# Gated delta rule: the small triangular inverses of both directions in one block, with half as many products per level

## The reference

```python
def gated_delta_chunked(q, k, v, g, beta):
    ...
    G = jnp.cumsum(g, axis=-1)
    decay = jnp.where(incl, jnp.exp(diff), 0.0)
    kb = k * beta[..., None]
    a = jnp.where(strict, jnp.einsum('bhnid,bhnjd->bhnij', kb, k) * decay, 0.0)
    rhs = jnp.concatenate([v * beta[..., None], kb * jnp.exp(G)[..., None]], axis=-1)
    sol = lax.linalg.triangular_solve(a, rhs, left_side=True, lower=True, unit_diagonal=True)
    ...
    def step(state, inp):
        v_new = u_c - jnp.einsum('bhck,bhkv->bhcv', w_c, state)
        o_c = (jnp.einsum('bhck,bhkv->bhcv', qd_c, state)
               + jnp.einsum('bhij,bhjv->bhiv', intra_c, v_new))
        state = (state * jnp.exp(gl_c)[..., None, None]
                 + jnp.einsum('bhck,bhcv->bhkv', kd_c, v_new))
        return state, o_c
...
    o_fwd = gated_delta_chunked(qh, kh, vh, gh[0], bh[0])
    o_bwd = flip(gated_delta_chunked(flip(qh), flip(kh), flip(vh), flip(gh[1]), flip(bh[1])))
```

## Time and profile before

| what | us |
|---|---|
| median of 3 runs (lowest, highest) | 3313.6 (3311.71, 3314.68) |
| the profiled execution, its own time | 3314.71 |
| its span in the trace | 3312.9 |
| mean granted clock of PE, share of full speed | 0.964 |
| busy PE / PEld / DVE / ACT / POOL | 3097.8 / 2499.8 / 1645.6 / 1044.2 / 1142.9 |
| gdn_chunks, from its first instruction on POOL to the next stage | 225 to about 555 |

### The profile page before, as it was taken

The page is one execution under the profiler, slowest core; times in us unless marked ns, Lnnn a source line. Parts: engine busy times, 40 slices in busy tenths (PEclk is TensorE's granted clock), DMA queues, the critical chain, the costliest instruction groups (busy, mean ns, idle before and its releaser), DMA issues. The chain is left out here.

```text
span 3312.9 us, 55513 instructions
## 1 busy us (share of the span) xinstructions
PE 3097.8 (94%) x21758; PEld 2499.8 (75%) x21758; DVE 1645.6 (50%) x2424; ACT 1044.2 (32%) x1584; POOL 1142.9 (34%) x542
## 2 busy tenths in 40 slices
PE   8977887999999989999899899999999979999998
PEld 6845676788878767888578688888888544589987
DVE  7834443422131345421477657655555667367741
ACT  4322322312331443222331333222223434343332
POOL 4432211444444214444222022222232247534443
PEclk9988888999999989999899999999999989999999
DMA  4224334223223112232311111111111111122222
GB/s 146 94 96 169 125 112 167 88 95 96 100 89 115 51 34 94 90 100 96 105 46 56 56 52 63 63 63 63 64 63 58 49 42 44 43 82 89 95 89 82
DMA packets 80204, 275.49 MB, mean 83 GB/s; under 512 B 9500, under 2 KB 12380, under 8 KB 79291
## 3 DMA queue, kind: packets, MB, share of 16 engines
q1 hardware_dynamic: 79771, 273.14, 25.2%
q10 hardware_dynamic: 288, 0.30, 0.0%
HBM read 263.41 MB, written 2.12 MB: 80 GB/s over the span
## 5 line engine op out<-in xcount | busy, mean ns | idle before, releaser
L207 POOL TENSOR_TENSOR weights_low<-weight_ring,weights_high 128x1024 fp32r<-128x1024 f32 x363 | 900.3, 2480 | 1637.5 <-ACT weights_high L201 1637.5
L201 ACT ACTIVATE weights_high<-weight_ring 128x1024 fp32r<-128x1024 f32 x377 | 397.6, 1055 | 859.0 <-PE bank L268 854.3
L266 PE MATMUL bank<-ffn_in_high,weights_low 128*128 128x258 f32 (+2 forms) x1552 | 488.2, 315 | 5.5 <-DVEq L2805 2.8
L268 PE MATMUL bank<-ffn_in_high,weights_high 128*128 128x258 f32 (+2 forms) x1552 | 487.9, 314 | 0.0
L267 PE MATMUL bank<-ffn_in_low,weights_high 128*128 128x258 f32 (+2 forms) x1552 | 487.7, 314 | 0.0
L266 PEld LDWEIGHTS bank<-ffn_in_high,weights_low 128*128 128x128 f32 x1552 | 294.8, 190 | 24.6 <-DVEq L2805 3.4
L267 PEld LDWEIGHTS bank<-ffn_in_low,weights_high 128*128 128x128 f32 x1552 | 295.2, 190 | 17.8
L268 PEld LDWEIGHTS bank<-ffn_in_high,weights_high 128*128 128x128 f32 x1552 | 294.0, 189 | 17.4
L266 PE MATMUL bank<-mlp_in_high,weights_low 128*128 128x512 f32 x496 | 194.6, 392 | 1.2 <-POOL weights_low L207 1.2
L267 PE MATMUL bank<-mlp_in_low,weights_high 128*128 128x512 f32 x496 | 193.2, 390 | 0.0
L266 PE MATMUL bank<-mlp_down_high,weights_low 128*128 128x512 f32 x496 | 193.1, 389 | 0.0
(11 more groups left out here) (671 smaller groups left out, 6474.5 us busy)
## 6 DMA issues: line engine op xcount, KB each, us to landing
weight_ring<-in_mod SPq DMA_DIRECT2D x96, 512.0 KB, 4.4
weight_ring<-in_ffn_up SPq DMA_DIRECT2D x88, 512.0 KB, 3.4
weight_ring<-in_mlp_up SPq DMA_DIRECT2D x64, 512.0 KB, 3.4
weight_ring<-in_mlp_down SPq DMA_DIRECT2D x64, 512.0 KB, 3.4
weight_ring<-in_ffn_down SPq DMA_DIRECT2D x44, 512.0 KB, 3.5
weight_ring<-in_gdn_in SPq DMA_DIRECT2D x32, 512.0 KB, 3.5
weight_ring<-in_dswa_in SPq DMA_DIRECT2D x27, 512.0 KB, 3.4
weight_ring<-in_fh_in SPq DMA_DIRECT2D x16, 512.0 KB, 3.5
```

Of the source, the lines that this page charges most:

```text
L201: act.activation(self.high[:, (g.s0 + at) % SPLIT, 0:g.floats], raw, ACT.Copy).then_inc(self.high_ready, 1)
L207: pool.tensor_tensor(self.low[:, slot, 0:g.floats], self.ring[:, (g.c0 + at) % RING, 0:g.floats], self.high[:, slot, 0:g.floats], ALU.subt ...
L266: pe.matmul(bank, wl, ah, start=start, stop=False)
L268: return pe.matmul(bank, wh, ah, start=False, stop=stop)
```

## The change

The strictly lower triangle of a forward block and the strictly upper triangle of the matching backward block are added into one 32x32 block (`B_joint`, As), so that 8 instead of 16 small matrices go through the levels. A table (`Tri.joined`) picks the entries of a level in both triangles. One joint array V (Y_joint) and its block transpose VX (X_joint) take the place of Y and X. The operands of the products, Yc and Xc, are V and VX multiplied by 0/1 tables (`of_y`, `of_x`) that keep, in each row, the triangle that belongs to it at that level. At the end `both_turned` splits VX into the two directions (Xd, 512 columns), and `widen` picks its direction out of V with a table.

The core of the diff (without the tables' construction, the tile declarations and the joins, in which only the index of Xc and Yc changes from m to s):

```diff
 level_q (PE), level_p (PE):
-                    for m in range(MATS):
+                    for m in range(SLOTS):
                         for b in range(4):
-                            last = pe.matmul(mats(LA[:, :])[quad(b), m, :], Am[quad(b), lv % 2, m, :], Yc[quad(b), m, :], start=True, stop=True)
+                            last = pe.matmul(mats(LA[:, 0:HALF])[quad(b), m, :], Am[quad(b), lv % 2, m, :], Yc[quad(b), m, :], start=True, stop=True)
 keep_q, keep_diagonal, small_blocks (ACT):
-                    act.activation(Q[:, :], LA[:, :], ACT.Copy).then_inc(q_ready, 1)
+                    act.activation(Q[:, 0:HALF], LA[:, 0:HALF], ACT.Copy).then_inc(q_ready, 1)
-                    act.wait_ge(x_ready, LV * p + LV)
+                    act.wait_ge(xd_ready, p + 1)
                     for b in range(4):
-                        last = act.activation(Xfull[quad(b), :, quad(b)], Xc[quad(b), :, :], ACT.Copy)
+                        last = act.activation(Xfull[quad(b), :, quad(b)], Xd[quad(b), :, :], ACT.Copy)
-                        act.wait_ge(masked, LV * p)
+                        act.wait_ge(joined, p)
 POOL:
+                def join_directions(p):
+                    pool.wait_ge(picked, 2 * p + 2)
+                    if p:
+                        pool.wait_ge(masked, LV * p)
+                    pool.tensor_tensor(As[:, :, :], Ac[:, of_d(0), :], Ac[:, of_d(1), :], ALU.add).then_inc(joined, 1)
-                    pool.tensor_tensor(Am[:, lv % 2, :, :].rearrange("p (d s) n -> p d s n", d=2), Ac[:, :, :].rearrange("p (d s) n -> p d s n", d=2),
-                                       level[:, :, lv, :].unsqueeze(2).broadcast_to([P, 2, SLOTS, SMALL]), ALU.mult).then_inc(masked, 1)
+                    pool.tensor_tensor(Am[:, lv % 2, :, :], As[:, :, :], by_slot(level.joined(lv)), ALU.mult).then_inc(masked, 1)
                 def widen(p):
-                        pool.tensor_copy(Yw[quad(b), :, b % 2 * SMALL:(b % 2 + 1) * SMALL], Yc[quad(b), of_d(b // 2), :]).then_inc(y_spread, 1)
+                        pool.tensor_tensor(Yw[quad(b), :, b % 2 * SMALL:(b % 2 + 1) * SMALL], V[quad(b), :, :],
+                                           by_slot(level.of_y(LEVELS + 1))[quad(b), :, :], ALU.mult).then_inc(y_spread, 1)
 DVE:
+                def choose_y(p, lv):
+                    dve.wait_ge(v_ready, LV * p + lv)
+                    dve.tensor_tensor(Yc[:, :, :], V[:, :, :], by_slot(level.of_y(lv)), ALU.mult).then_inc(y_ready, 1)
+                def choose_x(p, lv):
+                    dve.wait_ge(vx_ready, LV * p + lv)
+                    dve.tensor_tensor(Xc[:, :, :], VX[:, :, :], by_slot(level.of_x(lv)), ALU.mult).then_inc(x_ready, 1)
                 def level_up(p, lv):
                     dve.wait_ge(p_sums, NL * p + lv)
-                    dve.tensor_tensor(flat(Yc), flat(Yc), LB[:, :], ALU.subtract).then_inc(y_ready, 1)
-                    dve.wait_ge(y_ready, LV * p + lv + 1)
-                    dve.transpose(flat(Xc), flat(Yc)).then_inc(x_ready, 1)
+                    dve.tensor_tensor(flat(V), flat(V), LB[:, 0:HALF], ALU.subtract).then_inc(v_ready, 1)
+                    choose_y(p, lv + 1)
+                    dve.transpose(flat(VX), flat(V)).then_inc(vx_ready, 1)
+                    choose_x(p, lv + 1)
+                def both_turned(p):
+                    if p:
+                        dve.wait_ge(x_act, p)
+                    dve.tensor_tensor(Xd[:, :, :].rearrange("p (d s) n -> p d s n", d=2), VX[:, :, :].unsqueeze(1).broadcast_to([P, 2, SLOTS, SMALL]),
+                                      level.of_d().unsqueeze(2).broadcast_to([P, 2, SLOTS, SMALL]), ALU.mult).then_inc(xd_ready, 1)
```

More of the change, by code:

```diff
@@ L1047, in keep, with __init__, joined, of_y @@
         self.kept += 1
+class Tri:
+    COUNT = 3 * LEVELS + 3
+    def __init__(self, tables):
+        self.tables = tables
+    def joined(self, l):
+        return self.tables[:, l, :]
+    def of_y(self, l):
+        return self.tables[:, LEVELS + l - 1, :]
+    def of_x(self, l):
+        return self.tables[:, 2 * LEVELS + l, :]
+    def of_d(self):
+        return self.tables[:, 3 * LEVELS + 1:3 * LEVELS + 3, :]
 def gdn_chunks_stage(core, conv, gates, gate_z, masks, g_mod, silu, mod_columns, scratch):
@@ L1180, in level_p @@
                     pe.wait_ge(q_ready, NL * p + lv)
-                    for m in range(MATS):
+                    for m in range(SLOTS):
                         for b in range(4):
-                            last = pe.matmul(mats(LB[:, :])[quad(b), m, :], Xc[quad(b), m, :], Qm[quad(b), m, :], start=True, stop=True)
+                            last = pe.matmul(mats(LB[:, 0:HALF])[quad(b), m, :], Xc[quad(b), m, :], Qm[quad(b), m, :], start=True, stop=True)
                     last.then_inc(p_sums, 1)
@@ L1192, in join_32 @@
                                 a, b, m = first(d, h), second(d, h), d * SLOTS + s
-                                last = pe.matmul(slots(LA[:, 0:HALF])[quad(b), s, :], Bfull[quad(a), m, quad(b)], Yc[quad(a), m, :], start=True, stop=True)
+                                last = pe.matmul(slots(LA[:, 0:HALF])[quad(b), s, :], Bfull[quad(a), m, quad(b)], Yc[quad(a), s, :], start=True, stop=True)
                     last.then_inc(w5_sums, 1)
@@ L1202, in join_32_end @@
                             for d in range(2):
-                                a, b, m = first(d, h), second(d, h), d * SLOTS + s
-                                pe.matmul(slots(LB[:, 0:HALF])[quad(a), s, :], W5[quad(b), s, :], Xc[quad(b), m, :], start=True, stop=True)
+                                a, b = first(d, h), second(d, h)
+                                pe.matmul(slots(LB[:, 0:HALF])[quad(a), s, :], W5[quad(b), s, :], Xc[quad(b), s, :], start=True, stop=True)
                         for d in range(2):
-                            b, m = second(d, d), d * SLOTS + s
-                            last = pe.matmul(slots(LA[:, HALF:2 * HALF])[quad(b), s, :], Xc[quad(b), m, :], W5[quad(b), s, :], start=True, stop=True)
+                            b = second(d, d)
+                            last = pe.matmul(slots(LA[:, HALF:2 * HALF])[quad(b), s, :], Xc[quad(b), s, :], W5[quad(b), s, :], start=True, stop=True)
                     last.then_inc(x5_sums, 1)
@@ L1747, in _ @@
                         level_up(l, 4)
+                        both_turned(l)
                     if early:
@@ L3468, in gdn_constants @@
     r, c = r % SMALL, c[:, 0:SMALL]
-    half = lambda x, l, n: x // (1 << l) % 2 == n
-    level = np.stack([np.stack([(r // (2 << l) == c // (2 << l)) & half(r, l, d) & half(c, l, 1 - d) for l in range(LEVELS)], 1)
-                      for d in range(2)], 1).astype(np.float32)
+    late = lambda l: np.arange(P)[:, None] // (1 << l) % 2 == 1
+    joined = [(r // (2 << l) == c // (2 << l)) & (late(l) != (c // (1 << l) % 2 == 1)) for l in range(LEVELS)]
+    of_y = [np.where(late(l), c >= r, c <= r) for l in range(1, LEVELS + 2)]
+    of_x = [np.where(late(l), c >= r, c <= r) for l in range(1, LEVELS + 1)]
+    tables = np.stack(joined + of_y + of_x + [c >= r, c <= r], 1).astype(np.float32)
+    assert tables.shape[1] == Tri.COUNT
     eye = (r == c).astype(np.float32)
-    return np.ascontiguousarray(np.concatenate([x.reshape(P, -1) for x in (tri, negm, level, eye)], 1))
+    return np.ascontiguousarray(np.concatenate([x.reshape(P, -1) for x in (tri, negm, tables, eye)], 1))
 def buckets_of(rel):
```

33 lines of the change are left out of this document (20 added, 13 removed).

## The result

The changed kernel takes 3257.28 us (median of 4 runs, 3254.37 to 3258.96) against 3313.36 us of the kernel before beside it (4 runs): the ratio is 0.9827, with a 95% interval of 0.9815 to 0.9838. Two later sets of five runs gave 3257.53 and 3257.02. The forecast was 3260, with a range of 3246 to 3288. The profiled execution took 3258.96 us, with a span of 3257.2.

A forecast was written before the change was run, and what follows sets the result against it. PE was taken as bound by instruction supply, about 4.1 us per 128 pairs. Middles of 94.3 + 9.0 - 2.0 = 101.3 us, 54.0 less than 155.3, turn 3314.7 into 3260.7; less 1.1 gives 3260 us (range 3246 to 3288).

The forecast's parts named there:

- The supply of instructions: PE gets its program in pieces of about 128 load-and-multiply pairs, 4.14 us a piece, and stands still when faster.
- The middles: Rounds 1 to 4, first level product to join_32: forecast to fall from 155.3 to 101.3 us together.
- Round 1, by pieces: Round 1's stretch from first level product to join_32: 622 pairs at 4.14 us per 128, so 20.1 us.
- PE's work in rounds 2 to 4: PE's busy time from first level product to join_32, less half the level products: 25.9, 23.9 and 24.4 us.
- the clock: Part of PE's time ran at the 1.2 GHz level; fewer gaps should bring back 2 us (0 to 8).
- Idle time in rounds 2 to 4: Per round 1.7 us of remaining gaps and 1.3 of new scan waits, 3.0 together: 9.0 us for three rounds.
- What is late next: In rounds 2 to 4 pieces are nearly as slow as PE's work: 23 against 24 to 26 us.
- The new waits on the scan's places: state_changes(1), state_outputs(2) and state_changes(2) lose cover for DVE work: 1.3 us a round (0 to 2.3).
- Added operations: New DVE multiplications at 0.41 us, both_turned at 1.0, POOL masks at half of 1.27, dearer widen covered.
- rival 2: The levels' chain becomes the bound: two more DVE operations a level, possibly waiting for POOL, give back 21 us: 3281; chance 0.14.
- Rival 1: PE's gaps have another cause and stay; only the products' own 25.1 us goes: 3289 us; chance 0.12.
- rival 3: PE falls to the 1.2 GHz level for rounds 1 to 4: 58 us slower, 3372 us; chance 0.03.

The follow-up runs named there:

- The ffn_in groups: Changed kernel with 11 additional 32 x 32 products behind each of 147 groups of large products in the ffn_in stage: 3335.4 us.
- the run with half the instructions again: Changed kernel with each level product issued as 16 program products of 64 moving columns instead of 32 of 32: 3241.95 us.
- the run without choices: Changed kernel without the 40 DVE multiplications that choose the triangle, PE reading V and VX directly: 3252.64 us over 10 runs.
- the doubled and halved runs: Changed kernel, level products issued twice: 3318.62 us; kernel before, half the level products: 3256.39 us, or the same columns in half the instructions: 3260.49 us.

## Why the prediction was right

**The supply of instructions.** Right as a mechanism. 128 pairs from gap to gap, 5 transfers for 9, the whole gain with PE's stream alone, and none of it with the number of instructions restored. Of its size: 4.14 us a piece was the mean of middles that also held other work; added pieces cost 3.8 us, and bare ones stand 3.45 to 3.73 us apart. "One about every 4 us" is a mean too: single pieces come 3.30 to 5.25 us apart, with a transfer of 0.88 to 1.48 us in each.

**The Trainium skill's rule** that crossing a block of 256 instructions is "mostly hidden" ("Runtime: NRT & Kernel Launch", instruction fetch mechanics) does not describe these stretches: with 12.4 ns a pair a piece runs in 1.6 us and the next comes 3.3 to 5.25 us after the one before it. The ffn_in groups, at 0.12 us an instruction pair and with 0.2 us of issue ahead of L299 in all, agree with it, though most of them stand in loops, for which few pieces were fetched.

**The middles, 101.3 forecast, 96.5 measured.** Three terms make the 4.8 us. Round 1, by pieces: 20.1 against 19.7. PE's work in rounds 2 to 4: 25.9 + 23.9 + 24.4 - 2.0 = 72.2 against 24.7 + 23.4 + 21.7 = 69.8. The products' own halving came as worked out (50.2 us to 25.4), so the 2.4 us are time of the other instructions, and it goes with the clock, for which 2 of a possible 8 us were taken: it came back to 0.94, 1.00 and 1.00, and in round 4's middle a new_values record fell from 365 ns in the mean (L1255) to 288 (L1281). Idle time in rounds 2 to 4: 9.0 against 2.8 + 0.5 + 3.7 = 7.0. It was put in evenly, and falls unevenly: round 3 has no gap of supply at all.

**What is late next.** That PE's own work, no longer the supply, bounds rounds 2 to 4 was the prediction's, and the run with half the instructions again bears it out (15 us and not 30). The new waits on the scan's places are below the 1.3 us a round that were put in for them, 0.9 us on v_rest in all; the 4 to 5 us of the run without choices are not in the stage's end, and what they are is open.

**Added operations.** A 256-column step on DVE was taken at 0.41 us and is 0.42 to 0.44; Y is ready 0.86 us behind the product, for 0.82 forecast. both_turned is 1.21, for 1.0. POOL's masks of 256 columns took 0.73 us in the mean and B_joint as much, not half of 1.27; the three ahead of the first product make 2.2 us, still under the 2.5 of before. The fear that each multiplication waits for a mask of POOL did not come true: their longest is 0.68 us, their means 0.44, so rival 2's 21 us fall. widen hid as said; the ends of rounds 1 to 3 are 12.9, 16.3 and 17.6 us, from 12.2, 16.6 and 17.5.

**The sum and the rivals.** 54.0 us were forecast, 58.8 came in the middles, about 60 in the stage and 56.1 in the medians. That 3257.28 lies within 3 us of 3260 is in part luck: the middles came out 4.8 us better than the sum, and in two of three profiles some 3 us were lost behind the stage, where the sum had nothing. Rival 1 (3289) falls with the doubled and halved runs and with the transfers that end the gaps; rival 3 (3372) with a clock that rose in every middle.

## What to carry to other kernels

Where TensorE stands in "issue" with no wait in the program, count its records between the gaps: in these traces an even 127 or 128 (or twice that), whatever stood between, went with a supply of instructions that was the bound, and the gap ended soon after an instruction transfer had landed. Then fewer instructions are worth more than shorter ones, even at the price of additional work on another engine, and the test is cheap: issue the dense products twice and half as often, and look whether the time follows the count. Once the pieces take no longer than the engine's own work, less comes back: here 15 us for the last halving, where the supply alone would have given 30. A second profile of the same kernel tells which small differences are none.

## What the runs showed beyond that

- A 32x32 product of 64 moving columns took 17.8 ns a record in a stream (20.5 ns in the changed kernel's shorter bursts), one of 32 columns 12.4 ns.
- 22 small records between large ones cost 0.24 us beyond their own time, 0.27 at the median group.
- An instruction transfer of 16384 bytes took 0.88 to 1.48 us in rounds 1 to 4 of the kernel before, and PE went on 1.20 to 1.53 us after it had landed.
- The 512-column both_turned took 1206 ns in the changed kernel, 878 with widen as a copy, and 833 without the choices though widen was the two-source form there. The rule of the Trainium skill on DVE and POOL excluding each other for a whole instruction ("SBUF — State Buffer", "SBUF: two separate sides") does not order the three: POOL read SBUF in all of them, and without the choices both_turned started at 390.69 us, in the middle of a POOL operation from 390.25 to 390.97, and was the shortest. The cause is open.
